# The exits of the second block's three sub-layers in two ranges of 256 tokens

## The chip, the cores and the metric

The kernel runs on one core of a Trainium2 chip. The metric is the device time of one execution in microseconds (us). TensorE (PE, with its weight loads as PEld), VectorE (DVE), ScalarE (ACT) and GpSimd (POOL) each work through their own instructions in order and wait for each other through semaphores. SyncE (SP) issues the weight transfers.

## The reference

A float32 model on 512 tokens of width 1024 (`D`), two blocks of two layers each. What matters here is the second block. Each of its layers has three sub-layers: a gated feed-forward network of width 2816, a token mixer (a state-space part and attention), and a second feed-forward network.

```
def pre(x_in, i):
    return rms_norm(x_in, norm_pre[l, i]) * (1.0 + mod[:, i, 1]) + mod[:, i, 0]
def post_add(x_in, y, i, res_w):
    return x_in + res_w * mod[:, i, 2] * rms_norm(y, norm_post[l, i])
x = post_add(x, swiglu(pre(x, 0), ffn_w_in[l, 0], ffn_w_out[l, 0]), 0, FFN_RES)
y = token_mixer(pre(x, 1), ...)
x = post_add(x, y, 1, 1.0)
x = post_add(x, swiglu(pre(x, 2), ffn_w_in[l, 1], ffn_w_out[l, 1]), 2, FFN_RES)
```

Both norms take, for each token, a mean of squares over all 1024 channels. So the last of the eight output tiles of a sub-layer must be there before the root of any token is known.

## The kernel before

The activations lie with channels on the partitions: `xT` is 8 tiles (index k or m) of 128 channels x 512 tokens. A matrix product in near-float32 is three matmuls for each pair of 128x128 weights and 128x512 activations (`mm3`, lines 166 to 168: low weights with high activations, high with low, high with high). The split activations of a sub-layer's input are `xh` and `xl`. The weights come in blocks of up to 1024 columns through a ring of four slots: SP fetches (L136), ScalarE makes the high part (`hi`, L150), GpSimd subtracts it for the low part (`w_lo`, L160), TensorE uses the slot and raises `ring.used`.

An exit is what lies between the last output product of a sub-layer and the first products of the next. There are six: three in each layer, and the last of them has no next sub-layer. Its steps are these.

- TensorE makes output tile m = 0 to 7 into a PSUM bank. A feed-forward tile is 22 triples of matmuls (4 weight blocks of 6, 6, 5 and 5 triples), a mixer tile 8 triples (one block).
- For each tile ScalarE (`take_y`, L2140 to L2143) writes `y` (scaled), `ysq` and `sqt` (squares); VectorE multiplies `ycr` = y * xT (`cross`, L2419) and adds the products of the tiles before the last into `tot_ycr`, `tot_ysq`, `tot_sq` (`added`, L2378 and L2430). `y_added` counts this.
- TensorE sums totals and last tile over the partitions with a matrix of ones (`last_sums`, `sums`, L1852), 512 tokens in four groups of 128 which land in 32 partitions each.
- ScalarE takes the root (L2147), VectorE the reciprocal (L2464), TensorE spreads it over all partitions (`spread_root`, L1861). From the same sums VectorE works out the mean square of the new x in five small operations (L2468 to L2474), then root (L2155), reciprocal (L2476) and spread once more for the next sub-layer's input norm.
- For each tile k VectorE runs four operations of 512 columns: `part` (y times spread root, from PSUM, L2481), `added` (into xT, L2493), `scaled` (L2500, into `th_s`) and `low` (L2458, into `xl`); between the last two ScalarE writes `xh` (`shift`, L2164). The order is part, added, scaled of tile k+1 and then low of tile k. `low` raises `h_split`.
- TensorE starts the next sub-layer's first four weight columns (`products`): for k = 0 to 5 all four banks, then bank by bank k = 6 and 7. It waits for `h_split` at each new k, and frees the ring's slots with k = 7.

ScalarE's order at a feed-forward exit is: `hi` of the next sub-layer's weight blocks 0 to 2, `take_y` of tile 7, root, root, `hi` of block 3, shifts. In the first feed-forward network of a layer VectorE also prepares constants of the state-space part between the tiles (`prepare`).

Of the kernel before, what the change touches and what calls it, by code (L numbers as in the profile page):

```python
# [13 lines left out]
P = 128  # L14
# [210 lines left out]
def first_block(nc, block, mem, consts, own, prev, after, bank, xT, xh, xl, l, w_in, g_q, w_q_up, g_kv, w_kv_up,  # L225
# [1183 lines left out]
    "h_high", "y_added", "out_turned", "out_written")  # L1409
# [8 lines left out]
class SecondSignals(Signals):  # L1418
# [3 lines left out]
    def __init__(self, nc, ctx, ring, tag, layer, mixer):  # L1422
        Signals.__init__(self, nc, ctx, ring, tag)
        self.s = {x: self.sem(x) for x in SECOND_SIGNALS}
        self.s.update(mixer)
        self.since = {x: n * layer for x, n in MIXER_SIGNALS.items()}
        self.bank_used = None


def second_block(nc, block, mem, consts, own, prev, after, carried, out, bank, xT, xh, xl, l, mod_b, norm_pre,  # L1430
# [6 lines left out]
    E0 = 0 if prev is None else 1  # L1437

# [107 lines left out]
    for label, b in (("sq0", 7), ("ysq0", 6), ("ycr0", 5), ("post0", 4), ("pre1", 7)):  # L1546
        hold(label, b)
# [45 lines left out]
    for label, b in (("sq1", 7), ("ysq1", 6), ("ycr1", 5), ("post1", 4), ("pre2", 7)):  # L1593
        hold(label, b)
    hold_loop("in1", range(4), FT // 2)
    hold_loop("out1", range(2), KT // 2)
    if after is None:
        hold("sq2", 7)
        hold("post2", 4)
        for k, b in enumerate((0, 1, 2, 3, 5, 6, 7, 0)):  # L1600
            hold(("out", k), b)
    else:
        hold("vec_next", 5)
        for label, b in (("sq2", 7), ("ysq2", 6), ("ycr2", 5), ("post2", 4), ("pre3", 7)):
            hold(label, b)
# [212 lines left out]
    def _(pe):  # L1818
# [16 lines left out]
        def products(labels, n0, x, x_lo, at, banks=None):  # L1835

            banks = banks or [free(pe, label) for label in labels]
            order = [(k, b) for k in range(KT - 2) for b in range(4)] + [(k, b) for b in range(4) for k in (KT - 2, KT - 1)]
            for k, b in order:
                if b == 0:  # L1840
                    pe.wait_ge(s["h_split"], at + k + 1)
                wh, wl = weights(n0 + b, b) if k == 0 else (ring.hi[b], ring.lo[b])
                cc = slice(k * P, k * P + P)
                last = mm3(nc, banks[b], wh[:, cc], wl[:, cc], x[:, k, :], x_lo[:, k, :], k == 0, k == KT - 1)
                if k == KT - 1:
                    last.then_inc(ring.used, 1)
# [8 lines left out]
        def spread_root(n, label, r):  # L1855

            out = free(pe, label)
            pe.wait_ge(s["root_ready"], n)
            for g in range(TT):
                one_row = ident[:, 32 * g:32 * g + 1].broadcast_to([P, P])  # L1860
                last = nc.tensor.matmul(out[:, g * P:(g + 1) * P], one_row, r, start=True, stop=True)  # L1861
            last.then_inc(s["root_spread"], 1)

        def entry_norm():
# [5 lines left out]
            spread_root(1, "pre0", pre_r)  # L1870

        def last_sums(i):

            pe.wait_ge(s["y_added"], 6 * i + 6)
            for label, x in ([("ysq", ysq), ("ycr", ycr), ("sq", sqt)] if i < EXITS else [("sq", sqt)]):
                sums(free(pe, f"{label}{i}"), tot[label], True, False)
            for label, x in ([("ysq", ysq), ("ycr", ycr), ("sq", sqt)] if i < EXITS else [("sq", sqt)]):
                if label == "sq":
                    pe.wait_ge(*taken(i, KT - 1))
                else:  # L1880
                    pe.wait_ge(s["y_square" if label == "ysq" else "y_cross"], 8 * i + KT)
# [18 lines left out]
        def ffn(sub):  # L1900
# [13 lines left out]
            products(None, B_IN[sub], xh, xl, 16 * sub, bank[0:4])  # L1914
            with nc.tensor.Fori(1, FT // 2) as i:
                hidden(i)
            for m in range(KT):
# [12 lines left out]
            exit_norm(2 * sub)  # L1930
# [3 lines left out]
        products([("u", t) for t in range(4)], B_U, xh, xl, 8)  # L1934
# [166 lines left out]
        for m in range(KT):  # L2101
            product(free(pe, ("mo", m)), B_MO + m, m % 4, KT, MH, ML, wait=s["merged"] if m == 0 else None, at=since["merged"]).then_inc(ring.used, 1)
        exit_norm(1)
        ffn(1)
        if after is None:
            for k in range(KT):
                pe.wait_ge(s["y_sum"], 8 * 2 + k + 1)
# [6 lines left out]
    def _(act):  # L2114
# [18 lines left out]
        def take_y(i, m, src):  # L2133
# [3 lines left out]
            elif m == 0 and i:  # L2137
                act.wait_ge(s["mean_ready"], i + 1 - E0)
# [10 lines left out]
        def exit_norm(i):  # L2149

            act.wait_ge(s["mean_ready"], i + 2 - E0)
            root(post_r, f"sq{i}")
            if i < EXITS:
                act.wait_ge(s["new_mean"], i + 1)
                nc.scalar.activation(pre_r, ms[:, :], ACT.Sqrt, bias=eps[:, 0:1]).then_inc(s["pre_std"], 1)  # L2155

        def shift(i, k):

            to, at = stage(i)
            if k < KT - 1:  # L2160
# [20 lines left out]
        def ffn(sub):  # L2181
# [20 lines left out]
            for m in range(KT):  # L2202
                n = b_of + 4 * m
                for b in range(4 if m < KT - 1 else 3):
# [14 lines left out]
            exit_norm(2 * sub)  # L2219
            hi(b_of + 4 * KT + 3)  # L2220

        if prev is None:
# [8 lines left out]
            shifts(0)  # L2231
        ffn(0)
        shifts(1)
# [120 lines left out]
        for m in range(KT):  # L2354
            act.wait_ge(ring.used, B_MO + m + 1)
            read(take_y(1, m, held(("mo", m))), ("mo", m))
            if m < KT - 1:
                hi(B_MO + 4 + m)
            if m == 0:
                sqrt_table()  # L2360
        exit_norm(1)
# [580 lines left out]
```

## Time and profile before

| what | value |
| --- | --- |
| median of 3 runs | 3354.19 us (3351.44 to 3356.36) |
| profiled execution, its own time | 3349.84 us |
| profiled execution, span | 3348.0 us |
| mean granted TensorE clock | 0.975 of full speed |
| TensorE / VectorE busy | 96% / 62% of the span |

The profile is of one execution. Times within it are microseconds from the start of the span. A matmul's record is longer than its share of the engine, because matmuls overlap; the distance from start to start is what counts.

### The profile page before, as it was taken

The numbers are of one execution on the slowest core, as the hardware profiler recorded it, in microseconds if no ns is written. First come the engines' busy times: TensorE is split into PE (matmuls) and PEld (weight loads), VectorE is DVE, ScalarE is ACT, GpSimd is POOL, SyncE is SP. The second block draws the span as 40 slices with busy tenths as digits, with TensorE's granted clock in tenths as the row PEclk, the third lists the DMA queues.
The fourth block names the chain that finished last, engine by engine and source line by source line (L and its number), as shares of the span: only waits on it lengthen the run. The fifth ranks groups of instructions, "written<-read, shape, count | busy, mean of one in ns | idle before, by whom it ended". The sixth has DMA issues, their size and how long they took to land.

```text
span 3348.0 us, 43790 instructions
## 1 busy us (share of the span) xinstructions
PE 3199.6 (96%) x16130; PEld 2534.0 (76%) x16130; DVE 2070.9 (62%) x2722; ACT 1162.9 (35%) x1798; POOL 1337.2 (40%) x569
## 2 busy tenths in 40 slices
PE   8999999999996999899998999999998999989998
PEld 6757787757775888787677888878887876878887
DVE  3777785777785445898377443464459964774422
ACT  3355323355323223333434222422233335332233
POOL 3402343402333445544153445634464531534454
PEclk9999999999997999999999999999998999999999
DMA  4524472624553332667142332333235871423332
GB/s 128 186 82 126 145 226 74 190 74 130 151 176 93 98 94 82 97 112 102 55 122 64 114 94 84 103 88 100 85 92 82 129 103 33 142 76 100 92 86 73
DMA packets 577892, 358.73 MB, mean 107 GB/s; under 512 B 50946, under 2 KB 528588, under 8 KB 577484
## 3 DMA queue, kind: packets, MB, share of 16 engines
q1 hardware_dynamic: 573908, 350.23, 40.7%
q10 hardware_dynamic: 3832, 6.42, 0.5%
q8 instruction: 102, 1.67, 0.2%
q14 instruction: 50, 0.41, 0.0%
HBM read 343.75 MB, written 10.49 MB: 106 GB/s over the span
## 4 chain that ended last, share of the span: by engine, by line
PE 57%; DVE 7%; DMA 2%; SPq 1%; POOL 1%; ACT 1%; issue 1%; ACTq 0%; POOLq 0%; DVEq 0%
PE bank L166 18%; PE bank L168 17%; PE bank L167 17%; DMA w_raw<-in_mix_w_in_dram 2%; SPq L1754 1%; POOL w_lo L160 1%; DVE xT L2493 1%; DVE w_s L2378 1%; PE bank L2059 1%; PE bank L2038 1%; PE bank L2071 0%; PE bank L2018 0%; DVE y_s L2481 0%; DVE th_s L2500 0%; PE bank L2034 0%
## 5 line engine op out<-in xcount | busy, mean ns | idle before, releaser
L160 POOL TENSOR_TENSOR w_lo<-w_raw,w_hi 128x1024 fp32r<-128x1024 f32 (+1 forms) x556 | 1329.2, 2396 | 1975.2 <-ACT w_hi L150 1972.4
L166 PE MATMUL bank<-xh,w_lo 128*128 128x512 f32 x2432 | 973.8, 400 | 47.2 <-DVE xl L2458 28.1
L167 PE MATMUL bank<-xl,w_hi 128*128 128x512 f32 x2432 | 955.7, 393 | 0.0
L168 PE MATMUL bank<-xh,w_hi 128*128 128x512 f32 x2432 | 955.6, 393 | 0.0
L150 ACT ACTIVATE w_hi<-w_raw 128x1024 fp32r<-128x1024 f32 (+1 forms) x556 | 566.1, 1021 | 781.6 <-PE bank L168 673.4
L166 PEld LDWEIGHTS bank<-xh,w_lo 128*128 128x128 f32 x2432 | 462.4, 190 | 162.2 <-issue 47.5
L167 PEld LDWEIGHTS bank<-xl,w_hi 128*128 128x128 f32 x2432 | 463.0, 190 | 98.4 <-issue 4.8
L168 PEld LDWEIGHTS bank<-xh,w_hi 128*128 128x128 f32 x2432 | 461.8, 190 | 98.5
L166 PE MATMUL bank<-HH_s,w_lo 128*128 128x512 f32 x704 | 274.2, 389 | 0.0
L168 PE MATMUL bank<-HH_s,w_hi 128*128 128x512 f32 x704 | 273.9, 389 | 0.0
L167 PE MATMUL bank<-HL_s,w_hi 128*128 128x512 f32 x704 | 273.9, 389 | 0.0
L2613 DVE TENSOR_TENSOR th_s<-th_s,bank 128x512 f32<-128x512 f32 x88 | 60.5, 688 | 317.1 <-PE bank L168 316.0
L2617 DVE SCALAR_TENSOR_TENSOR HL_s<-th_s,HH_s 128x512 f32 x88 | 242.6, 2756 | 10.9
L2189 ACT ACTIVATE th_s<-bank 128x512 f32<-128x512 f32 x88 | 52.7, 599 | 383.2 <-PE bank L168 353.7
L2610 DVE SCALAR_TENSOR_TENSOR th_s<-th_s,bank 128x512 f32<-128x512 f32 x88 | 60.5, 687 | 171.9 <-ACT th_s L2189 171.9
L1146 DVE SCALAR_TENSOR_TENSOR macc_b_l<-m_raw_l,cs_l,macc_b_l 128x512 f32<-128x512 f32 x168 | 160.8, 957 | 4.7
L167 PEld LDWEIGHTS bank<-HL_s,w_hi 128*128 128x128 f32 x704 | 132.2, 188 | 27.5
L166 PEld LDWEIGHTS bank<-HH_s,w_lo 128*128 128x128 f32 x704 | 132.2, 188 | 27.5
L168 PEld LDWEIGHTS bank<-HH_s,w_hi 128*128 128x128 f32 x704 | 132.2, 188 | 27.2
L2430 DVE TENSOR_TENSOR tot_sq_s<-tot_sq_s,sqt_s 128x512 f32<-128x512 f32 x36 | 89.9, 2496 | 94.1 <-ACT sqt_s L2143 93.1
L2419 DVE TENSOR_TENSOR ycr_s<-y_s,xT 128x512 f32<-128x512 f32 x35 | 48.6, 1389 | 112.8 <-ACT y_s L2140 112.6
L1146 DVE SCALAR_TENSOR_TENSOR macc_a_l<-m_raw_l,cs_l,macc_a_l 128x512 f32<-128x512 f32 x56 | 66.1, 1180 | 13.0 <-DMA m_raw_l<-in_mod_w_dram 11.2
(509 smaller groups left out, 4276.1 us busy)
## 6 DMA issues: line engine op xcount, KB each, us to landing
w_raw<-in_ffn_w_in_dram SPq DMA_DIRECT2D x176, 512.0 KB, 3.8
m_raw_l<-in_mod_w_dram SPq DMA_DIRECT2D x128, 512.0 KB, 5.0
w_raw<-in_w_in_dram SPq DMA_DIRECT2D x78, 512.0 KB, 4.0
w_raw<-in_mix_w_in_dram SPq DMA_DIRECT2D x64, 512.0 KB, 9.7
w_raw<-in_ffn_w_out_dram SPq DMA_DIRECT2D x64, 384.0 KB, 3.4
w_raw<-in_ffn_w_out_dram SPq DMA_DIRECT2D x64, 320.0 KB, 3.2
m_half_l<-in_mod_w_dram SPq DMA_DIRECT2D x32, 256.0 KB, 2.8
w_raw<-in_w_out_dram SPq DMA_DIRECT2D x16, 512.0 KB, 4.7
```

Source lines behind the costliest of these rows:

```text
L150: ins = nc.scalar.activation(to(ring.hi[s]), of(ring.raw[s]), ACT.Copy)
L160: ins = nc.gpsimd.tensor_tensor(to(ring.lo[s]), of(ring.raw[s]), to(ring.hi[s]).bitcast(F32), ALU.subtract)
L166: nc.tensor.matmul(out, wl, xh, start=start, stop=False)
L167: nc.tensor.matmul(out, wh, xl, start=False, stop=False)
L168: return nc.tensor.matmul(out, wh, xh, start=False, stop=stop)
L1146: ins = V.scalar_tensor_tensor(macc[:, :], w, cc, macc[:, :], ALU.mult, ALU.add)
L2189: nc.scalar.activation(th[v][:, :], bank[2 * v], ACT.Tanh, scale=0.5).then_inc(s["tanh"], 1)
L2419: V.tensor_tensor(to[:, :], y[:, m, :], xT[:, m, :], MUL).then_inc(s["y_cross"], 1)
L2430: V.tensor_tensor(tot["sq"][:, :], tot["sq"][:, :], sqt[m % 2][:, :], ADD).then_inc(s["y_added"], 1)
L2610: V.scalar_tensor_tensor(t[:, :], t[:, :], 1.0, bank[2 * v], ADD, MUL).then_inc(evac[2 * v], 1)
L2613: V.tensor_tensor(t[:, :], t[:, :], bank[2 * v + 1], MUL).then_inc(evac[2 * v + 1], 1)
L2617: V.scalar_tensor_tensor(HL[:, to, :], t[:, None, :], 0.5, HH[:, to, :].bitcast(F32), MUL, SUB).then_inc(s["hidden"], 1)
```

## The change

Everything at an exit that took 512 tokens now takes a range of 256 (`tok[0]`, `tok[1]`), once for each half `hf`.

- The last output tile (`TAIL` = 7) is made in two passes over the same weights, the first into its old bank and the second into another bank (`tail`). Sums, roots and spreads of half 0 are put between the matmuls of half 1.
- ScalarE takes the halves of the last tile with two sets of three operations. At a feed-forward exit `hi` of the next blocks 0 to 2 now comes after the first root: block 0 between the two roots of half 0, blocks 1 and 2 after them, block 3 between the shifts.
- The three sums share one bank. A spread is made for each half.
- VectorE runs part, added, scaled and low on 256 columns, all 8 tiles of half 0 and then all 8 of half 1. The last tile's second `cross_half`, the root work of half 1 (after tile 2) and its second reciprocal (after tile 4) stand between them.
- `products` goes through the 32 pairs of tile and weight column twice, with matmuls of 256 columns: for half 0 in an order in which columns 2 and 3 lag by one and two tiles, with the sums and spreads of half 1 of the exit behind steps 7, 15 and 23. The entry of the first layer goes in halves too.

```diff
 def products(labels, n0, x, x_lo, at, banks=None, tail=None):
...
+            for hf in range(2):
+                if hf == 0:
+                    order = sorted(((k, b) for k in range(KT) for b in range(4)), key=lambda kb: (kb[0] + (0, 0, 1, 2)[kb[1]], kb[1]))
+                else:
+                    order = [(k, b) for k in range(KT - 2) for b in range(4)] + [(k, b) for b in range(4) for k in (KT - 2, KT - 1)]
+                split = 0
+                for i, (k, b) in enumerate(order):
+                    if k + 1 > split:
+                        split = k + 1
+                        pe.wait_ge(s["h_split"], at + 8 * hf + split)
+                    wh, wl = weights(n0 + b, b) if k == hf == 0 else (ring.hi[b], ring.lo[b])
+                    cc = slice(k * P, k * P + P)
+                    last = mm3(nc, banks[b][:, tok[hf]], wh[:, cc], wl[:, cc], x[:, k, tok[hf]], x_lo[:, k, tok[hf]], k == 0, k == KT - 1)
+                    if hf and k == KT - 1:
+                        last.then_inc(ring.used, 1)
+                    if tail is not None and hf == 0 and i in (7, 15, 23):
+                        tail((i - 7) // 8)
...
 # TensorE, feed-forward exit
+            for hf in range(2):
+                out = free(pe, f"tail{i}") if hf else bank[TAIL % 2]
+                for b in range(4):
+                    wh, wl = weights(4 * TAIL + B_OF[sub] + b, b)
+                    for k in range(CUT[b], CUT[b + 1]):
+                        cc = slice((k - CUT[b]) * P, (k - CUT[b] + 1) * P)
+                        last = mm3(nc, out[:, tok[hf]], wh[:, cc], wl[:, cc], HH[:, k, tok[hf]], HL[:, k, tok[hf]], k == 0, k == FT - 1)
+                        if hf and (b, k - CUT[b]) == (3, 2):
+                            first_half(i, 2)
+                    if hf:
+                        last.then_inc(ring.used, 1)
+                        if b < 2:
+                            first_half(i, b)
...
 # TensorE, mixer exit
+        for hf in range(2):
+            out = free(pe, "tail1" if hf else ("mo", TAIL))
+            for k in range(KT):
...
+                if hf and k == 4:
+                    first_half(1, 0)
...
+        first_half(1, 1)
+        first_half(1, 2)
...
 # ScalarE
+        def exit_tail(i, src, splits, last, done):
+            take_half(i, 0, src)
+            post_root(i, 0)
+            for n in splits[0:1]:
+                hi(n)
+            if i < EXITS:
+                pre_root(i, 0)
+            for n in splits[1:3]:
+                hi(n)
+            act.wait_ge(ring.used, done)
+            take_half(i, 1, src)
...
+            shift(i + 1, 0, 0)
+            hi(last)
+            shift(i + 1, 0, 1)
+            shift(i + 1, 0, 2)
+            post_root(i, 1)
+            shift(i + 1, 0, 3)
+            shift(i + 1, 0, 4)
+            pre_root(i, 1)
...
 # VectorE
+            pre_root(i, 0)
+            dve.wait_ge(s["root_spread"], 1 - E0 + root_count(i, 1))
+            part(0, 0)
+            added(0, 0)
+            dve.wait_ge(s["root_spread"], 1 - E0 + root_count(i, 2))
+            scaled(0, 0)
+            cross_half(i, 1)
+            order = [(hf, k) for hf in range(2) for k in range(KT)]
+            for n, item in enumerate(order):
+                if n + 1 < len(order):
+                    if n + 1 == KT:
+                        dve.wait_ge(s["root_spread"], 1 - E0 + root_count(i, 4))
+                    part(*order[n + 1])
+                    added(*order[n + 1])
+                    scaled(*order[n + 1])
+                low(i + 1, *item)
+                if item == (0, 2):
+                    post_root(i, 1)
+                if item == (0, 4):
+                    pre_root(i, 1)
```

`first_half(i, step)` is, on TensorE, the sums (step 0), the first spread (1) and the second spread (2) of half 0; the `tail` argument does the same for half 1.

## Rows read from the trace of the kernel before

**Rows 1.** The page: engines and the chain that ended last.
```profile
PE 3199.6 (96%) x16130; PEld 2534.0 (76%) x16130; DVE 2070.9 (62%) x2722; ACT 1162.9 (35%) x1798; POOL 1337.2 (40%) x569
PE 57%; DVE 7%; DMA 2%; SPq 1%; POOL 1%; ACT 1%; issue 1%; ACTq 0%; POOLq 0%; DVEq 0%
```
**Rows 2.** TensorE's waits, whole span: total us, times, longest.
```profile
PE bank L166 <- DVE xl L2458: 28.1, 6, 5.5
...
PE bank L2059 <- ACT PT_s L2330: 10.7, 4, 5.3
```
**Rows 3.** Timeline of layer 0's first exit: start, duration, [idle before].
```profile
1403.84 2.82 DVE L2430 TENSOR_TENSOR tot_sq_s<-tot_sq_s,sqt_s 128x512 f32<-128x512 f32 x1
...
1404.80 0.39 PE L168 MATMUL bank<-HH_s,w_hi 128*128 128x512 f32 x1
...
1406.63 2.36 POOL L160 TENSOR_TENSOR w_lo<-w_raw,w_hi 128x1024 fp32r<-128x1024 f32 x1 [0.52 <-ACT w_hi L150]
...
1407.15 2.39 DVE L2419 TENSOR_TENSOR ycr_s<-y_s,xT 128x512 f32<-128x512 f32 x1 [0.49 <-ACT y_s L2140]
...
1410.70 0.95 DVE L2464 RECIPROCAL rstd_s<-rstd_s 128x128 f32<-128x128 f32 x1 [1.17 <-ACT rstd_s L2147]
...
1413.69 0.95 DVE L2476 RECIPROCAL rstd_s<-rstd_s 128x128 f32<-128x128 f32 x1 [0.47 <-ACT rstd_s L2155]
...
1421.53 0.76 PE L166 MATMUL bank<-xh,w_lo 128*128 128x512 f32 x1 [4.70 <-DVE xl L2458]
```
**Rows 4.** VectorE's timeline, one round of the loop over tiles.
```profile
1425.40 0.75 DVE L2500 SCALAR_TENSOR_TENSOR th_s<-xT,pre_s,bank 128x512 f32<-128x512 f32 x1
1426.07 0.75 DVE L2458 SCALAR_TENSOR_TENSOR xl<-th_s,modc,xh 128x512 fp32r<-128x512 f32 x1
1426.73 0.68 DVE L2481 TENSOR_TENSOR y_s<-y_s,bank 128x512 f32<-128x512 f32 x1
1427.44 0.69 DVE L2493 TENSOR_TENSOR xT<-xT,y_s 128x512 f32<-128x512 f32 x1
1428.17 0.75 DVE L2500 SCALAR_TENSOR_TENSOR th_s<-xT,pre_s,bank 128x512 f32<-128x512 f32 x1
```
**Rows 5.** VectorE's groups by shape: operations of 256 columns; busy, mean ns.
```profile
L2378 DVE TENSOR_TENSOR b_s<-fr_s,Bi_s 128x256 f32<-128x256 f32 x2 | 5.0, 2506 | 0.1
...
L2378 DVE TENSOR_TENSOR b_s<-fi_s,Bi_s 128x256 f32<-128x256 f32 x2 | 0.9, 426 | 0.1
```
**Rows 6.** Timeline at full clock: eight weight loads of a spread, their eight matmuls.
```profile
1806.68 0.97 PEld L1861 LDWEIGHTS bank<-rstd_s,tables_sb 128*128 128x128 f32 x8 [1.81 <-issue]
1806.71 1.13 PE L1861 MATMUL bank<-rstd_s,tables_sb 128*128 128x128 f32 x8 [1.57 <-DVE rstd_s L2464]
```
**Rows 7.** Last totals at a mixer exit and at layer 0's last exit (timeline).
```profile
1800.45 2.83 DVE L2430 TENSOR_TENSOR tot_sq_s<-tot_sq_s,sqt_s 128x512 f32<-128x512 f32 x1
...
2169.12 2.77 DVE L2430 TENSOR_TENSOR tot_sq_s<-tot_sq_s,sqt_s 128x512 f32<-128x512 f32 x1
```
**Rows 8.** Output matmuls of those exits by source line; first and last start.
```profile
L168 PE MATMUL bank<-MH_s,w_hi x19: 388/389/389, 1790.2 to 1802.5; 128*128 128x512 f32 x19
...
L168 PE MATMUL bank<-HH_s,w_hi x27: 388/389/389, 2160.3 to 2177.9; 128*128 128x512 f32 x27
```
**Rows 9.** The chain of work: first products, their end, the next weights.
```profile
1445.09 0.87 PE bank L1939 x8
...
1816.44 0.77 PE bank L166
...
1838.13 2.41 POOL w_lo L160
...
2191.89 0.77 PE bank L166
```
**Rows 10.** VectorE's timeline in the mixer, its longest wait before attention.
```profile
1545.39 0.69 DVE L2730 COPY Xr_s<-rho_s 128x1024 f32<-128x1024 f32 x1 [2.72 <-PE bank L2002]
```
**Rows 11.** Stretch of the first products: us, engines' busy time, granted clock (PEclk).
```profile
1421.50:1425.00 3.50, 3.47 (x9) 2.78 (x10) 3.40 (x6) 0.73 (x1) 0.00 (x0) 0.54 0.87 197
```

More of the change, by code:

```diff
@@ L1833, in product, with products @@
             return last
-        def products(labels, n0, x, x_lo, at, banks=None):
+        def products(labels, n0, x, x_lo, at, banks=None, tail=None):
             banks = banks or [free(pe, label) for label in labels]
[L1838 to L1846, printed above, removed]
+            for hf in range(2):
[15 more added lines that the diff above has]
+                        tail((i - 7) // 8)
         def sums(out, x, start, stop):
@@ L1853, in sums, with spread_half @@
             return last
[L1855 to L1861, printed above, removed]
+        def spread_half(hf, label, r):
+            out = free(pe, f"{label}{hf}")
+            h = rows_of[hf]
+            for g in (2 * hf, 2 * hf + 1):
+                one_row = ident[h, 32 * g:32 * g + 1].broadcast_to([P // 2, P])
+                last = nc.tensor.matmul(out[:, g * P:(g + 1) * P], one_row, r[h, :], start=True, stop=True)
             last.then_inc(s["root_spread"], 1)
@@ L1913, in ffn @@
                     pe.wait_ge(prev.evac[b], prev.bank_used[b])
-            products(None, B_IN[sub], xh, xl, 16 * sub, bank[0:4])
+            products(None, B_IN[sub], xh, xl, 32 * sub, bank[0:4],
+                     second_half(1) if sub else prev.tail if prev is not None else None)
             with nc.tensor.Fori(1, FT // 2) as i:
                 hidden(i)
-            for m in range(KT):
+            for m in range(TAIL):
                 pe.wait_ge(evac[m % 2], m // 2 + turn[f"out{sub}"][m % 2])
@@ L2218, in ffn @@
                     sqrt_table()
-            exit_norm(2 * sub)
-            hi(b_of + 4 * KT + 3)
+            n = b_of + 4 * TAIL
+            exit_tail(2 * sub, bank[TAIL % 2], [n + 4 + b for b in range(3)], n + 7, n + 4)
         if prev is None:
@@ L2230, in _ @@
                 hi(B_IN[0] + n)
-            shifts(0)
+            for hf in range(2):
+                for k in range(KT):
+                    shift(0, hf, k)
         ffn(0)
-        shifts(1)
         for t in range(4):
@@ L2633, in ffn @@
                 if part < EXITS:
-                    cross(part, m)
+                    if m == TAIL:
+                        cross_half(part, 0)
+                    else:
+                        cross(part, m)
                 if part == 2 and m == 0 and after is not None:
```

340 lines of the change are left out of this document (221 added, 119 removed).

## Prediction

> **What bounds the kernel now.** I read the page first: TensorE is busy 96% of the span, and the chain that ended last is mostly its matmuls; VectorE is busy 62% [rows 1]. So only what adds or removes TensorE time, or holds TensorE up, counts. Then TensorE's waits: the longest is for `low` (`xl`), 28.1 us in 6 waits, the entry and the five exits that have a next sub-layer [rows 2]. The timeline of one exit shows a serial chain: last matmul, ScalarE, sums, root, reciprocal, root, reciprocal, part, added, scaled, shift, low, first product [rows 3].
>
> I count from T, the start of the last output tile. Matmuls of 512 columns follow each other every 0.227 us (26 triples from 2160.3 to 2177.9, 18 from 1790.2 to 1802.5 [rows 8]); a feed-forward tile takes 66 x 0.227 = 15.0 us, a mixer tile 5.45. T is 1390.05 at a layer's first exit (A), 1797.3 at the mixer exit (B), 2163.15 at layer 0's last (C) [rows 3, 8]. The first product starts at T+31.5, T+19.1 and T+28.7 [rows 3, 9]. There are two A, two B, one C, and the last exit D without a next input.
>
> The next four columns then take 23.6 us, 1421.53 to 1445.09 [rows 3, 9], of which 96 matmuls, 21.8 us at 0.227, are TensorE's own work. VectorE feeds them at the distances 0.67, 0.66, 0.71 and 0.73 us, 2.77 us for each tile [rows 4], against 12 x 0.227 = 2.72 us of TensorE. They are level. That balance is what the change touches.
>
> **TensorE's price of halves.** No row has a split-precision matmul of 256 columns. Below it is half of 0.227, 0.114 us. Above it is 0.227, if weight loads of 128 columns could not go faster. Against that: eight loads with their eight matmuls follow at (0.97 - 0.19)/7 = 0.111 us [rows 6]. Keeping the fixed part of 0.227, I take 0.120: a feed-forward tail grows from 15.0 to 15.8 us, a mixer tail from 5.45 to 5.8, the four columns from 21.8 to 23.0.
>
> The Trainium skill (TensorE: Matmul & The Clock Gate, Back-to-back issue gap) gives N/2.4 + 2.5 ns, 109 ns for 256 columns. By it my sum below would be some 5 us less.
>
> **VectorE's price of halves.** An operation of 256 columns takes 0.426 us where 512 take 0.69 [rows 4, 5]: 0.265 less, not half. Each of the four distances shrinks by 0.267, so a half tile costs 2.77 - 1.07 = 1.70 us against 12 x 0.120 = 1.44 us on TensorE. VectorE becomes the pacer. Sixteen half tiles, from the first `low` to the last: 14 x 1.70 + 0.4 = 24.2 us. In between, new in this place:
> - after `low` of tile 2, VectorE waits for half 1's sums, which TensorE reaches only behind three more triples: 1.1 + 0.2 + sums 0.7 + root and hand-overs 0.6 = 2.6 us;
> - reciprocal 0.95 and the five mean operations, 3.0 us from reciprocal to reciprocal less 0.45 for the root [rows 3]: 2.5 us;
> - the second reciprocal: 1.0 us;
> - before half 1, the last spread, behind step 23: 1.1 + 0.2 + 0.45 + 0.15 = 1.9 us;
> - after the last `low`, seven triples on TensorE: 0.2 + 21 x 0.120 = 2.7 us.
> The sum is 24.2 + 2.6 + 2.5 + 1.0 + 1.9 + 2.7 = 34.9 us against 23.6: **+11.3 us** at each of five exits. ScalarE's shifts lie beside this (0.5 of each 1.70 us). TensorE waits meanwhile and hides its own surcharge.
>
> **When the columns start.** At A the totals of tile 6 end at 1406.66 = T+16.6 [rows 3], because `prepare` holds VectorE. The new half sums stand behind the first block of half 1 (T+10.1), so TensorE waits there and the tail ends near T+25, no longer T+15. Sums, root and reciprocal end at T+19.1, the second reciprocal 3.0 us later, and part, added, scaled, the second cross (which needs `take_half` behind two `hi` of 1.06 us) and the first round bring the first product to T+27.5. At C the totals are ready (2171.9 = T+8.7 [rows 7]); the same steps give T+20.4. At B they are ready at 1803.3 = T+6.0 [rows 7], behind which the same chain gives T+15.4: a short tail hides little.
>
> These times suppose that GpSimd is not in the way. It is: an operation of VectorE with two SBUF operands that starts while GpSimd splits weights takes 2.39 us and ends 0.55 after it [rows 3], and the same form of 256 columns takes 2.506 instead of 0.426 [rows 5]: 2.1 us lost for each meeting. Before, three of the four splits lay beside the long tail. Now `hi` of blocks 0 to 2 comes after the first root, so all four (2.4 us each) fall on the mean operations, `added`, cross and `low`. Bounds: none met (+0) and three to four effective (+6.0 at A and C), one at B (+2.2). I take two thirds at A and C and the one at B: starts T+31.5, T+24.5, T+17.6, against T+31.5, T+28.7, T+19.1. So the start gains 0, 4.2 and 1.5 us.
>
> The Trainium skill (SBUF — State Buffer, Terms) has VectorE and GpSimd share a port pair that is held for the full instruction, the loser blocked. If every overlap costs as it says, A and C start 2 us later and the sum is some 6 us more.
>
> **Other terms.**
> - At A the mixer's VectorE work begins later: the last `low` ends at T+63.7 (31.5 + 34.9 - 2.7), before at T+48.8 (31.5 - 0.2 and 6 x 2.77 + 0.9 for the seven other tiles). Of these 14.9 us a wait of 2.72 [rows 10] takes up; then attention waits for VectorE's chain already (10.7 us of TensorE's waits are behind it [rows 2]). So A costs 12.2, not 11.3.
> - The ring: before, column 0 was done 6 triples (4.1 us) ahead of the end, and `hi` 1.06 plus `w_lo`, ending at 1840.54 [rows 9], just fill that. Now it is 6 half triples, 2.2 us: TensorE waits 1.9 us more at B (two), C and the entry; at A the transposes of 0.87 [rows 9] cover half, 1.0.
> - The entry: 1.2 more on TensorE, 0.7 earlier start: +0.5.
> - D: tail +0.8, half 0's sums and spread on TensorE +0.9, shorter chain for half 1 -1.1, VectorE's extra operation for each of eight tiles (2 x 0.426 - 0.69 = 0.16) +1.2: +1.8.
> - More semaphores and one bank for three sums: nothing, they lie beside.
>
> **Sum.** A 2 x 12.2 = 24.4; B 2 x (11.3 - 1.5) = 19.6; C 11.3 - 4.2 = 7.1; ring 4 x 1.9 + 2 x 1.0 = 9.6; entry 0.5; D 1.8: +63.0. B's and C's columns took some 0.4 more than A's before (a longer slow stretch), 1.2 in all: **+62 us**. The profiled execution took 3349.84, 4.35 below the median; on the median 3354.2 + 62 = **3416 us**.
>
> **Rivals.**
> 1. *GpSimd is rarely met*: the bound of none. 2 x 4.0 + 4.1 + 2 x 2.2 = 16.5 less: 3400. For it: which operation gets in first is a matter of tenths of a microsecond. Against: three of the four `hi` have their data early.
> 2. *All splits meet, and the clock falls.* TensorE at the first products had 0.54, the 1.2 GHz level, for 3.5 us after it had been mostly waiting [rows 11]. Cold halves cost 0.213 instead of 0.120, and the 24 ahead of half 1's sums lengthen VectorE's wait by 1.6 us in five places. With 6 us of splits: +14, 3430.
> 3. *VectorE does not pace*: faster. If a half tile took VectorE under 1.44 us and half 1's roots were met ready, the columns would take TensorE's 23.0 us; then only the starts count, 4.2 + 2 x 1.5 earlier plus 16.5 without meetings, less ring, entry and D, 11.9: 12 us faster, 3342. The point is 1.44 us a half tile. Against: four times 0.36 is below any such operation in the rows.
> 4. *Weight loads bind* at 0.19 to 0.227 for 256 columns: tails longer by up to 14 us and columns by TensorE's 40 us instead of 34.9: near 3510. Against: 0.111 in rows 6.
> 5. *It cancels*: earlier starts at all exits and little waiting inside the columns leave the time within 0.2%.
>
> **How the numbers follow.** Forecast 0.50, rival 1 0.20, rival 2 0.15, rival 3 0.07, rival 4 0.04, cancelled 0.04. About 0.2% (7 us) is what a measurement of this kernel can tell from no change. Faster 0.07, same 0.04, slower 0.89. The range holds the first three: below, rival 1 with halves at 0.114 and no ring wait, 3400 - 5 - 10 and some 5 for the waits inside the columns, 3380; above, rival 2 and as much again of slow clock, 3440.
>
> **What would show it.** Between the first half product and the last, VectorE's four operations near 1.70 us a round and TensorE idle a good part; a VectorE wait of some 2.6 us after the third `low`; operations of 256 columns with 2 us and more beside GpSimd's splits; half matmuls 0.12 us apart; at A the half sums waiting for `tot_sq`. I am wrong if the rounds take under 1.5 us, if TensorE's waits for `xl` fall below 28.1 us in total, or if the columns take under 30 us.

## The result, and the profile after

The changed kernel took 3424.66 us (median of 4 runs, 3420.72 to 3427.28) against 3353.29 (3351.44 to 3356.36): ratio 1.0211, 95% interval 1.0193 to 1.0229. It is 71.4 us slower; 62 were forecast, 3416 us, in a range of 3380 to 3440. Its profiled execution took 3423.56 us with a span of 3421.8, 73.8 more than the span before.

The page, engines and the chain that ended last, answers to [rows 1]:
```profile
PE 3246.0 (95%) x17018; PEld 2612.3 (76%) x17018; DVE 2118.8 (62%) x2947; ACT 1183.9 (35%) x1874; POOL 1342.7 (39%) x569
...
PE 54%; DVE 14%; issue 1%; ACT 1%; POOL 0%; DMA 0%; ACTq 0%; POOLq 0%; DVEq 0%
```
VectorE's busy share is still 62%, but its share of the chain went from 7% to 14%: a share of busy time did not show this, the chain does. TensorE's waits over the span (total us, times, longest), against [rows 2]:
```profile
PE bank L166 <- DVE xl L2602: 62.7, 20, 7.2
...
PE bank L166 <- POOL w_lo L160: 17.1, 11, 4.3
...
PE bank L1903 <- DVE tot_sq_s L2569: 7.2, 4, 2.3
PE bank L2065 <- ACT Btr_s L2424: 6.9, 2, 3.9
...
PE bank L2136 <- ACT PT_s L2468: 1.2, 4, 0.4
```
The kernel before had, beside the waits of [rows 2]:
```profile
PE bank L166 <- POOL w_lo L160: 7.1, 6, 4.3
...
PE bank L1852 <- DVE tot_sq_s L2430: 3.9, 4, 1.5
```
The wait for `low` has more than doubled and comes 20 times instead of 6. The wait for GpSimd's `w_lo` went from 7.1 to 17.1 us. The half sums inside the tail wait for `tot_sq`, as forecast, 7.2 us in 4 waits. The 10.7 us ahead of attention have shrunk to 1.2, but 6.9 us of waiting for `Btr_s`, a table of the state-space part, are new in the mixer.

VectorE's timeline at layer 0's first exit (A1; the two layers' exits are A1, B1, C, then A2, B2 and the last, D), against [rows 3, 4] (T, the start of the last output tile, is 1396.64 here):
```profile
1408.34 0.69 DVE L2569 TENSOR_TENSOR tot_sq_s<-tot_sq_s,sqt_s 128x512 f32<-128x512 f32 x1
1409.06 0.42 DVE L2558 TENSOR_TENSOR ycr_s<-y_s,xT 128x256 f32<-128x256 f32 x1
1411.79 0.94 DVE L2611 RECIPROCAL rstd_s<-rstd_s 64x128 f32<-64x128 f32 x1 [2.30 <-ACT rstd_s L2257]
...
1413.40 1.98 DVE L2511 TENSOR_TENSOR ms_t_s<-ms_t_s,rstd_s 64x128 f32<-64x128 f32 x1
...
1417.68 2.48 DVE L2681 TENSOR_TENSOR xT<-xT,y_s 128x256 f32<-128x256 f32 x1
...
1420.67 1.98 DVE L2558 TENSOR_TENSOR ycr_s<-y_s,xT 128x256 f32<-128x256 f32 x1
...
1423.01 2.12 DVE L2681 TENSOR_TENSOR xT<-xT,y_s 128x256 f32<-128x256 f32 x1
...
1425.56 0.48 DVE L2602 SCALAR_TENSOR_TENSOR xl<-th_s,modc,xh 128x256 fp32r<-128x256 f32 x1
...
1427.26 0.48 DVE L2602 SCALAR_TENSOR_TENSOR xl<-th_s,modc,xh 128x256 fp32r<-128x256 f32 x1
...
1428.96 0.48 DVE L2602 SCALAR_TENSOR_TENSOR xl<-th_s,modc,xh 128x256 fp32r<-128x256 f32 x1
1433.19 0.95 DVE L2611 RECIPROCAL rstd_s<-rstd_s 64x128 f32<-64x128 f32 x1 [3.75 <-ACT rstd_s L2257]
```
Read three things. The rounds of a half tile are 1.70 us apart (1425.56, 1427.26, 1428.96). Four operations, each with two SBUF operands, take 1.98 to 2.48 us, although 0.29 to 0.42 is their own time where no split runs beside them: the meetings with GpSimd's splits. And behind the third `low`, VectorE stands 3.75 us for half 1's sums. The rest of these columns (timeline of TensorE, with VectorE's wait for the last spread and ScalarE's first reading of column 0):
```profile
1426.29 0.55 PE L166 MATMUL bank<-xh,w_lo 128*128 128x256 f32 x1 [6.49 <-DVE xl L2602]
1426.64 0.41 PE L167 MATMUL bank<-xl,w_hi 128*128 128x256 f32 x1
...
1430.44 0.28 PE L166 MATMUL bank<-xh,w_lo 128*128 128x256 f32 x1
...
1437.58 0.58 PE L166 MATMUL bank<-xh,w_lo 128*128 128x256 f32 x1 [4.29 <-DVE xl L2602]
...
1446.02 0.42 DVE L2668 TENSOR_TENSOR y_s<-y_s,bank 128x256 f32<-128x256 f32 x1 [2.28 <-PE bank L1881]
...
1461.11 0.60 ACT L2375 ACTIVATE us_s<-bank 128x512 f32<-128x512 f32 x1 [1.23 <-PE bank L168]
...
1463.07 1.03 PE L2016 MATMUL bank<-tables_sb,crow_s 128*128 128x128 f32 x8
```
The first 17 half matmuls follow at 0.21 us, then the distance falls to 0.12. The stretches show why (us, busy times of the engines, granted clock, DMA share, GB/s), against [rows 11]:
```profile
1426.30:1430.30 4.00, 4.00 (x17) 3.82 (x18) 3.00 (x8) 0.51 (x1) 0.00 (x0) 0.50 0.98 59
1430.30:1431.20 0.90, 0.90 (x8) 0.80 (x7) 0.00 (x0) 0.00 (x0) 0.00 (x0) 0.99 0.48 75
```
A granted clock of 0.50 is the 1.2 GHz level, after 6.49 us of waiting; half 1's sums stand behind just these matmuls. At the other four exits the slow level lasts longer: 9.0, 5.6, 6.1 and 8.1 us from the first product (B1, C, A2, B2), so that nearly all of the 24 matmuls ahead of those sums run at it, and it comes back after the later waits inside the columns.

At A1 the four columns take 1426.29 to 1463.07, 36.8 us; 23.6 before, 34.9 forecast. That is the exit nearest to the forecast: B1, C, A2 and B2 took 41.2, 38.1, 38.3 and 40.6 us, where they had taken 23.9 each. For the table one mark serves all exits: from T to ScalarE's first reading of column 0's products, in two parts, to the first product and from there. It comes from the timelines of both kernels. The kernels of the experiments are in the same table.

| kernel | A1 | B1 | C | A2 | B2 |
|---|---|---|---|---|---|
| before | 31.5 + 19.5 | 19.2 + 20.0 | 28.7 + 20.0 | 31.8 + 20.0 | 19.2 + 20.0 |
| after | 29.7 + 34.8 | 16.0 + 39.2 | 26.6 + 36.1 | 29.0 + 36.3 | 15.6 + 38.6 |
| vector_in_halves | 32.5 + 23.6 | 19.3 + 23.6 | 28.8 + 23.6 | 32.0 + 23.6 | 19.3 + 23.6 |
| sums_ahead | 28.8 + 28.9 | 15.4 + 30.7 | 26.4 + 29.0 | 29.4 + 29.0 | 15.9 + 34.7 |
| one_operation_less | 27.9 + 25.6 | 15.9 + 26.7 | 25.5 + 25.6 | 27.8 + 25.6 | 15.3 + 29.8 |
| after_no_low | 24.5 + 37.5 | 14.5 + 35.8 | 22.2 + 36.3 | 24.5 + 34.7 | 14.2 + 34.9 |
| before_no_low | 30.4 + 20.4 | 17.4 + 19.5 | 27.8 + 20.2 | 28.5 + 20.0 | 18.3 + 20.2 |
| columns_whole | 37.4 + 19.7 | 25.4 + 20.7 | 32.5 + 20.1 | 36.2 + 19.6 | 27.1 + 20.2 |
| whole_spreads_late | 35.2 + 20.8 | 24.7 + 20.4 | 32.7 + 19.9 | 36.4 + 19.4 | 24.5 + 19.5 |
| one_root | 31.7 + 19.9 | 19.9 + 20.0 | 31.0 + 20.5 | 31.7 + 20.3 | 19.9 + 20.1 |

The first product comes 2 to 4 us sooner after the change, and everything behind it 15 to 19 us later. Sums against before: A +13.5 twice, B +16.1 and +15.0, C +14.1, 72.2 in all. Between A's first reading and B's T there are 353.75 and 352.17 us instead of 356.24 and 356.78, 7.1 back. The last exit is +2.2, the entry's first column +2.3 from its first product. The first product of the entry is 4.3 later, and that is not the change's: ScalarE's root there starts at 1037.99 instead of 1033.38, ahead of the first instruction that was changed, and lies between 1030.8 and 1038.9 in the profiles of this study. 72.2 - 7.1 + 2.2 + 2.3 + 4.3 = 73.9: but for rounding the difference of the spans, 73.8.

### The profile page after: what moved, and what is told of

It reads as the page before. It is cut to its first block, busy times and chain, and to the rows that moved or that the text cites. A ratio compares the mean times of both kernels' runs of the same rounds, so it can differ in the third digit from the quotient of the medians.

```text
span 3421.8 us, 45914 instructions
## 1 busy us (share of the span) xinstructions
PE 3246.0 (95%) x17018; PEld 2612.3 (76%) x17018; DVE 2118.8 (62%) x2947; ACT 1183.9 (35%) x1874; POOL 1342.7 (39%) x569
## 4 chain that ended last, share of the span: by engine, by line
PE 54%; DVE 14%; issue 1%; ACT 1%; POOL 0%; DMA 0%; ACTq 0%; POOLq 0%; DVEq 0%
PE bank L166 17%; PE bank L168 16%; PE bank L167 16%; DVE w_s L2511 2%; DVE xT L2681 1%; DVE ct_s L2511 1%; DVE tt_s L2511 1%; DVE z_s L2511 1%; DVE tot_sq_s L2569 1%; PE bank L2115 1%; PE bank L2136 1%; DVE xl L2602 1%; PE bank L1903 1%; PE bank L2095 1%; DVE th_s L2688 1%
## 5 line engine op out<-in xcount | busy, mean ns | idle before, releaser
L166 PE MATMUL bank<-xh,w_lo 128*128 128x512 f32 (+1 forms) x2624 | 1019.6, 389 | 91.4 <-DVE xl L2602 62.7
L167 PE MATMUL bank<-xl,w_hi 128*128 128x512 f32 (+1 forms) x2624 | 997.3, 380 | 0.0
L168 PE MATMUL bank<-xh,w_hi 128*128 128x512 f32 (+1 forms) x2624 | 996.7, 380 | 0.0
L166 PEld LDWEIGHTS bank<-xh,w_lo 128*128 128x128 f32 x2624 | 509.3, 194 | 203.4 <-issue 53.0
L167 PEld LDWEIGHTS bank<-xl,w_hi 128*128 128x128 f32 x2624 | 510.4, 195 | 90.3 <-issue 5.1
L168 PEld LDWEIGHTS bank<-xh,w_hi 128*128 128x128 f32 x2624 | 509.4, 194 | 89.9
L166 PE MATMUL bank<-HH_s,w_lo 128*128 128x512 f32 (+1 forms) x792 | 291.3, 368 | 0.0
L167 PE MATMUL bank<-HL_s,w_hi 128*128 128x512 f32 (+1 forms) x792 | 289.8, 366 | 0.0
L168 PE MATMUL bank<-HH_s,w_hi 128*128 128x512 f32 (+1 forms) x792 | 289.7, 366 | 0.0
L2810 DVE SCALAR_TENSOR_TENSOR HL_s<-th_s,HH_s 128x512 f32 x88 | 242.5, 2756 | 10.9
L168 PEld LDWEIGHTS bank<-HH_s,w_hi 128*128 128x128 f32 x792 | 149.8, 189 | 23.9
L2277 ACT ACTIVATE xh<-th_s,modc 128x256 fp32r<-128x256 f32 x96 | 48.8, 509 | 134.6 <-DVE th_s L2688 124.4
```

Of the source, the lines that this page charges most:

```text
L166: nc.tensor.matmul(out, wl, xh, start=start, stop=False)
L167: nc.tensor.matmul(out, wh, xl, start=False, stop=False)
L168: return nc.tensor.matmul(out, wh, xh, start=False, stop=stop)
L2810: V.scalar_tensor_tensor(HL[:, to, :], t[:, None, :], 0.5, HH[:, to, :].bitcast(F32), MUL, SUB).then_inc(s["hidden"], 1)
```

## The experiments

**1. VectorE and ScalarE in halves, in the kernel before.**
```diff
+    pieces = [(k, hf) for k in range(KT) for hf in range(2)]
...
-                    pe.wait_ge(s["h_split"], at + k + 1)
+                    pe.wait_ge(s["h_split"], 2 * (at + k + 1))
...
+            for n, item in enumerate(pieces):
+                if n + 1 < len(pieces):
+                    part(*pieces[n + 1])
+                    added(*pieces[n + 1])
+                    scaled(*pieces[n + 1])
+                low(i + 1, *item)
```


> The kernel before, with only VectorE's and ScalarE's work behind each root (part, added, scaled, shift, low) in operations of 256 columns, tile by tile; roots, sums and TensorE's matmuls stay whole. My theory (VectorE paces the first four columns, 1.70 us for a half tile): 16 rounds where 8 of 2.77 us were, so some 5 us more at each of five exits, a little less at the two ahead of attention: about 3378 us (3370 to 3388), with TensorE's waits for low near 50 us. The rival that VectorE does not pace: within 5 us of before, 3353 to 3358.

Measured: 3378.41 us, 1.0074 (1.0057 to 1.0090), 26 us more. VectorE's rounds (timeline) and TensorE's waits:
```profile
1427.26 0.48 DVE L2464 SCALAR_TENSOR_TENSOR xl<-th_s,modc,xh 128x256 fp32r<-128x256 f32 x1
1427.65 0.41 DVE L2488 TENSOR_TENSOR y_s<-y_s,bank 128x256 f32<-128x256 f32 x1
1428.10 0.42 DVE L2501 TENSOR_TENSOR xT<-xT,y_s 128x256 f32<-128x256 f32 x1
1428.56 0.48 DVE L2509 SCALAR_TENSOR_TENSOR th_s<-xT,pre_s,bank 128x256 f32<-128x256 f32 x1
1428.96 0.48 DVE L2464 SCALAR_TENSOR_TENSOR xl<-th_s,modc,xh 128x256 fp32r<-128x256 f32 x1
```
```profile
PE bank L166 <- DVE xl L2464: 43.5, 24, 5.7
```
Roots, sums and matmuls are as before, and 3.6 to 4.1 us are lost between first product and first reading at each exit. A further 3.2 us are lost at each A between that reading and B's T, where a wait of TensorE's for `Btr_s`, 2.9 us, is new. TensorE's waits for `low` are 43.5 us, for some 50 expected. So the size of the operations behind the roots (VectorE's four, and ScalarE's shift with them) alone costs some 25 of the 71 us.

**2. The changed kernel with whole columns.**
```diff
-            for hf in range(2):
...
+                for n in range(3):
+                    tail(n)
...
+            for k, b in order:
...
+            post_root(i, 0)
...
+                pre_root(i, 0)
+                cross_half(i, 1)
+            post_root(i, 1)
...
+                pre_root(i, 1)
```


> The changed kernel with its last output tile, sums and roots in two ranges kept, but the normalised tiles and the first four columns whole again, behind both ranges' roots. My theory: the columns fall from some 37 us back to 23.6, while the start moves back behind half 1's roots (about 13 us behind the end of the tail): start at T+36, T+20.5 and T+32 at A, B and C against T+31.5, T+19.1 and T+28.7 before, +15 in all, and the last exit +2: about 3370 us (3360 to 3380). The rival that the split tail itself carries the loss: 3400 or more.

Measured: 3377.85 us (3366.34 to 3383.43), 1.0067 (1.0043 to 1.0092): 47 us less than the changed kernel. The columns are back at some 20 us to the first reading; the starts stand at T+37.4, T+25.4 and T+32.5, later than I expected at B by 5. TensorE waits for roots inside the tail, which puts the tail's end off; experiment 8 asks whether that is what holds the start.

**3. Half 1's sums ahead of the products, in the changed kernel.**
```diff
+            if tail is not None:
+                tail(0)
             for hf in range(2):
...
-                    if tail is not None and hf == 0 and i in (7, 15, 23):
-                        tail((i - 7) // 8)
+                    if tail is not None and hf == 0 and i in (12, 16):
+                        tail((i - 8) // 4)
```


> The changed kernel with half 1's sums ahead of the first half product instead of behind eight triples, and its two spreads behind the triples 13 and 17 instead of 16 and 24. If the waits inside the columns (3.75 to 5.2 us for the sums of half 1, 2.3 to 3.1 us for the last spread) come from TensorE's order, they shrink to under 1 us each: 25 to 30 us less, about 3397 us (3390 to 3403). The rival that they come from the work on VectorE and ScalarE itself, and only change their name: 3415 to 3425.

Measured: 3391.18 us (3390.59 to 3394.20), 1.0114 (1.0097 to 1.0131), 33.5 us less than the changed kernel. VectorE's timeline at the place of the 3.75 us wait, and the wait for `low` over the span:
```profile
1430.83 0.48 DVE L2604 SCALAR_TENSOR_TENSOR xl<-th_s,modc,xh 128x256 fp32r<-128x256 f32 x1
1431.34 0.95 DVE L2613 RECIPROCAL rstd_s<-rstd_s 64x128 f32<-64x128 f32 x1
1432.32 0.29 DVE L2618 TENSOR_TENSOR ms_t_s<-bank,rstd_s 64x128 f32<-64x128 f32 x1
```
```profile
PE bank L166 <- DVE xl L2604: 27.1, 15, 3.8
```
The reciprocal follows its `low` at once. Nothing was made shorter, three items of TensorE's queue were moved: the waits were an effect of order. From first product to end the columns now take 30.9 us at A1, C and A2; the prediction's sum without its two waits is 34.9 - 2.6 - 1.9 = 30.4. The slow clock went back with the waits: 23 to 34 half matmuls of the columns run at the slow distance, where it had been 38 to 59, except at B2 with 57 of them, whose columns take 36.7 us. So some of the 33.5 us is clock.

**4. The price of half matmuls, in the kernel before.**
```diff
-                    product(bank[b], n, b, KT, xh, xl).then_inc(ring.used, 1)
+                    for c in (slice(0, T // 2), slice(T // 2, T)):
+                        for k in range(KT):
+                            last = mm3(nc, bank[b][:, c], wh[:, cc], wl[:, cc], xh[:, k, c], xl[:, k, c], k == 0, k == KT - 1)
```


> The kernel before, with the 40 weight blocks of each feed-forward loop that TensorE alone sets the time of (3840 matmuls of 512 columns in all) done as two runs of 256 columns, each with its own weight loads: a price for the half matmul. At my 0.120 us: 3840 x (0.240 - 0.227) = +50 us, 3403. At exactly half, 0.114: 3357. At 0.109: 3320. If weight loads bind at 0.19 to 0.227: 590 to 870 us more.

Measured: 3402.09 us (3401.02 to 3406.93), 1.0146 (1.0129 to 1.0163), 49.9 us more: 13.0 ns for each of the 3840 pairs. The timeline, start by start:
```profile
1100.13 0.28 PE L166 MATMUL bank<-xh,w_lo 128*128 128x256 f32 x1
1100.25 0.28 PE L167 MATMUL bank<-xl,w_hi 128*128 128x256 f32 x1
1100.37 0.28 PE L168 MATMUL bank<-xh,w_hi 128*128 128x256 f32 x1
```
The distance is 0.120 us at full clock. Weight loads of 128 columns do not bind at 256.

**5. One of VectorE's four operations less**, on top of the kernel of 3 (tiles 1 to 6 of each half leave out the addition of y to x).
```diff
             def added(hf, k):
+                if 0 < k < KT - 1:
+                    return
```


> The kernel with half 1's sums ahead (3391.18 us), where the tiles 1 to 6 of each half leave out VectorE's addition of y to x (the output differs), one of the four operations of a round: 3 x 0.426 = 1.28 us a round against TensorE's 1.44. If VectorE paces the half columns: 12 rounds x (1.70 - 1.44) = 3.1 us less at each of five exits, about 3376 us (3370 to 3380). If TensorE paces them, nothing changes: 3388 to 3394.

Measured: 3359.12 us (3355.44 to 3366.56), 32 us less than with the operation; against before 1.0025 (1.0014 to 1.0035). Both theories missed the size, and the direction is the first's. The rounds (timeline) are 1.12 us, shorter than TensorE's 1.44:
```profile
1423.14 0.48 DVE L2604 SCALAR_TENSOR_TENSOR xl<-th_s,modc,xh 128x256 fp32r<-128x256 f32 x1
1423.53 0.41 DVE L2670 TENSOR_TENSOR y_s<-y_s,bank 128x256 f32<-128x256 f32 x1
1423.86 0.47 DVE L2693 SCALAR_TENSOR_TENSOR th_s<-xT,pre_s,bank 128x256 f32<-128x256 f32 x1
1424.26 0.47 DVE L2604 SCALAR_TENSOR_TENSOR xl<-th_s,modc,xh 128x256 fp32r<-128x256 f32 x1
```
From first product to first reading it saves 3.3, 4.0, 3.4, 3.4 and 4.9 us, near the 3.1 expected. The rest lies in starts that are 0.9 to 1.5 us earlier at the feed-forward exits, and in 4.7 and 6.7 us between A's first reading and B's T: TensorE's waits there fall from 10.6 to 6.4 and from 10.9 to 5.4 us, above all those for `Btr_s` (3.9 and 4.2), which are gone. What VectorE finishes earlier at A helps the mixer behind it.

**6. and 7. GpSimd's splits cut to one column** at the four blocks behind each exit (`four` runs `split_lo` with `ONE_COLUMN`), in the changed kernel and in the one before.
```diff
+ONE_COLUMN = [(lambda x: x[:, 0:1], lambda x: x[:, 0:1])]
...
-        quads(4, B_G + 4)
+        quads(4, B_U)
+        four(B_U)
+        quads(B_U + 4, B_G + 4)
```


> The changed kernel, with GpSimd's low parts of the four weight blocks behind each exit cut to one column (this leaves out those low parts, so the output differs), TensorE's matmuls unchanged: it takes the meetings of VectorE with GpSimd away, and TensorE's waits for w_lo there. If all four splits cost some 2.1 us of the chain at A and C and one or two at B, as the trace reads: 3 x 7 + 2 x 3 us, and some 12 us of ring waits: about 3388 us (3378 to 3398). If the meetings lie beside other waits, only the ring waits go: 3410 or more.

> The same cut in the kernel before (again without those low parts), as the control: there one meeting at an exit lies on the chain (2.1 us at A and C), and TensorE waits 7.1 us for w_lo: about 3341 us (3335 to 3348). The meetings and ring waits that the change adds are then the difference of the two differences, by my reading some 25 us; by the rival under 8.

Measured: after 3401.59 us (3398.84 to 3403.76), 23.1 less; before 3342.42 (3337.68 to 3347.75), 10.3 less, 0.9972 (0.9960 to 0.9983). The first misses its range of 3378 to 3398, and neither expectation read the edit right. It leaves TensorE's waits for `w_lo` behind the columns, 1.2 to 2.1 us at each exit, as they were, since those are for the next four blocks. What it prices is the meetings alone: the change adds 12.8 us of them. In the kernel before I had counted one meeting on the chain at A and at C; its trace has more: the first `xT` at all five exits and the cross at both A, 1.7 us each, 12 us together, where the run gives 10.3 back. In the changed kernel the blocked operations lose 24 us together, and the run gives 23.1 back.

Exit by exit the two don't agree so well. The start moved by 4.4 to 5.1 us at A and C, where four operations had lost 6.9 together (at C: 1.67 + 2.02 + 1.56 + 1.69, each less its own 0.29 or 0.42), and by 1.4 to 1.5 at B. VectorE's operations did lose their 2 us: `xT` at C is 0.43. But VectorE then waits for TensorE's spread and for ScalarE's `y` (timelines of VectorE and TensorE at C):
```profile
2207.21 0.43 DVE L2692 TENSOR_TENSOR xT<-xT,y_s 128x256 f32<-128x256 f32 x1
2209.29 0.48 DVE L2699 SCALAR_TENSOR_TENSOR th_s<-xT,pre_s,bank 128x256 f32<-128x256 f32 x1 [1.66 <-PE bank L1892]
2210.71 0.42 DVE L2569 TENSOR_TENSOR ycr_s<-y_s,xT 128x256 f32<-128x256 f32 x1 [0.93 <-ACT y_s L2255]
...
2213.09 0.55 PE L166 MATMUL bank<-xh,w_lo 128*128 128x256 f32 x1 [2.92 <-POOL w_lo L160]
```
6.94 - 1.66 - 0.93 = 4.35, and the start moved by 4.4. The wait put down to `w_lo` is for block 3's `hi` on ScalarE; it ends only 0.15 us behind the first `low`.

**8. Whole columns, with half 0's spreads and all of half 1's sums and spreads behind the tail.**
```diff
                     if hf:
                         last.then_inc(ring.used, 1)
-                        if b < 2:
-                            first_half(i, b)
+                        if b == 0:
+                            first_half(i, 0)
...
+            second_half(i)(0)
+            for step in (1, 2):
+                first_half(i, step)
+            for step in (1, 2):
+                second_half(i)(step)
```


> As the kernel with split tail and whole columns (3377.85 us), but TensorE doesn't wait for half 0's roots inside the tail: half 0's spreads and all of half 1's sums and spreads stand behind the tail. There TensorE waited 23.8 us in 15 places for the roots, and the tail's end stood behind them. If that order moved the start back: about 3350 us (3343 to 3358), no slower than before. If the chain of two roots on VectorE is what sets the start: 3370 or more.

Measured: 3373.61 us (3363.91 to 3378.05), 1.0054 (1.0036 to 1.0073). My 3350 was wrong. The start moved by 2.2 us or less at four exits and by 2.6 at B2: T+35.2, 24.7, 32.7, 36.4 and 24.5. VectorE's timeline at the first exit says why:
```profile
1409.15 0.94 DVE L2592 RECIPROCAL rstd_s<-rstd_s 64x128 f32<-64x128 f32 x1 [1.62 <-ACT rstd_s L2253]
...
1413.81 0.94 DVE L2612 RECIPROCAL rstd_s<-rstd_s 64x128 f32<-64x128 f32 x1 [0.47 <-ACT rstd_s L2263]
1416.06 1.45 DVE L2545 TENSOR_TENSOR ycr_s<-y_s,xT 128x256 f32<-128x256 f32 x1 [1.31 <-ACT y_s L2240]
1418.86 0.95 DVE L2592 RECIPROCAL rstd_s<-rstd_s 64x128 f32<-64x128 f32 x1 [1.35 <-ACT rstd_s L2253]
...
1421.83 0.95 DVE L2612 RECIPROCAL rstd_s<-rstd_s 64x128 f32<-64x128 f32 x1 [0.46 <-ACT rstd_s L2263]
```
A reciprocal over 64 partitions takes 0.94 us, as long as one over 128 [rows 3]. Splitting by partitions halves nothing: half 1's chain is as long as the whole one was, and half 0's is extra.

**9. The split tail with one root**, to tell the split tail from the split roots: one set of sums behind the tail, one post root and one pre root. `both` is TensorE's sums and spreads over all 128 partitions. The edit also puts ScalarE's `hi` of three blocks back ahead of the second half's reading, so against experiment 8 two things differ.
```diff
-                            first_half(i, b)
...
+            both(i)
...
-            post_root(i, 0)
-            for n in splits[0:1]:
-                hi(n)
-            if i < EXITS:
-                pre_root(i, 0)
-            for n in splits[1:3]:
+            for n in splits:
                 hi(n)
             act.wait_ge(ring.used, done)
             take_half(i, 1, src)
+            post_root(i)
```


> The split tail alone: the last output tile in two ranges of 256 tokens and ScalarE's three reads of each, but one set of sums behind the tail, one post root and one pre root over all 128 partitions, whole tiles and whole columns. If it is the two chains of roots on VectorE, and TensorE's stop in the tail for half 0's sums, that put the start back by 4 to 5 us in the kernels with whole columns (T+35 to 37, T+24.5 to 27 and T+32.6 at A, B and C), the start comes to the tail's T+15.5 (B: 5.6) and 13.1 us of chain: T+28.6 to 29.5, T+18.7, T+28.6, and the time to 3345 to 3355 us, level with before. If the halved tail itself costs (its matmuls, its splits that come late), it stays at 3362 or more.

Measured in 11 runs against 15: 3352.64 us (3347.46 to 3355.64) against 3352.97, ratio 0.9999 (0.9990 to 1.0008): level with before. The starts missed at the feed-forward exits (T+31.7 and T+31.0; I had 28.6 to 29.5), with this in the way (VectorE's timeline at the first exit):
```profile
1405.58 4.99 DVE L2542 TENSOR_TENSOR ycr_s<-y_s,xT 128x256 f32<-128x256 f32 x2
1411.92 0.95 DVE L2589 RECIPROCAL rstd_s<-rstd_s 128x128 f32<-128x128 f32 x1 [1.35 <-ACT rstd_s L2256]
...
1416.44 2.43 DVE L2632 TENSOR_TENSOR xT<-xT,y_s 128x512 f32<-128x512 f32 x1
```
The two cross halves, 0.42 us each, took 4.99 us together: they met splits, which GpSimd ran from 1402.60 to 1410.30. In this form the split tail gains nothing, and it costs nothing that could be measured. That the splits fall there because the blocks of the ring come free only with half 1 is my reading of the order, not tested.

## Why the prediction was right

**VectorE paces the half columns: right.** 1.70 us a round, forecast 1.70; it costs 26 us alone (experiment 1), and taking an operation away shortens the columns by about the amount at which TensorE takes over (5). 256 columns take 0.42 us where 512 take 0.69. The Trainium skill (VectorE: DVE Perf Modes, The TRN2 errata) gives (N + 151)/0.96 ns for such an operation, 691 and 424 ns: the trace agrees, and a half keeps over 60% of the price.

**TensorE's price: right.** 0.120 us (4), so rival 4, that weight loads bind, is out. The 109 ns that the Trainium skill (TensorE: Matmul & The Clock Gate, Back-to-back issue gap) gives for 256 columns, as the gap of a matmul by itself, set against the measured 0.227 us of 512, would by estimate have made experiment 4 about 35 us faster than before; it was 49.9 slower.

**The columns: 34.9 forecast, 36.8 to 41.2 measured.** Two terms were too small. The wait for half 1's sums, 2.6, was 3.75, 5.24, 4.44, 4.62 and 4.82 (A1, B1, C, A2, B2); the wait for the last spread, 1.9, was 2.3 to 3.1. Over the five exits that is 13.6 us more than forecast. The slow clock of rival 2 is there, and longer than the rival had it. At A1 17 half matmuls at 0.213 instead of 0.120 are 1.6 us more ahead of those sums, the rival's own figure; at the other four nearly all 24 are slow, some 2 us. At B a meeting of VectorE with a split, 1.7 us, falls inside the columns too. No run changed the clock alone, so its share is read, not tested. That these waits are TensorE's order is shown (3): with the order changed they went but for one of 2.0 us at B2, and 33.5 us with them.

**The starts.** A was given no gain and had 1.8 and 2.8; B 1.5 and had 3.1 and 3.6; C 4.2 and had 2.1. The kernel without the splits (6) parts each start into chain and meetings. The chain alone was forecast at T+27.5, 15.4 and 20.4 (A, B, C) and came at T+24.5, 14.2 to 14.5 and 22.2; so it was 3.0 us too long at A, and 1.8 too short at C, where the run shows VectorE waiting 1.66 us for the spread and 0.93 for `y`. At A the totals of tile 6 ended at T+12.4, not T+16.6: ScalarE's `hi` had moved behind the first root, so GpSimd no longer sat on `tot_sq`, 0.69 us where it took 2.82 [rows 3]. I had moved those splits and left what they had blocked as it was. Starts, columns and the column's earlier end together, the first reading comes 13.5 us later at A (forecast 11.3 + 1.9 = 13.2), 15.0 to 16.1 at B (11.7) and 14.1 at C (9.0): 72.2 for a forecast of 58.8. That the total was nearer is in part luck: columns 20 us too short were set off by starts that came 6 us earlier than forecast and by 7 us in the mixer that I had with the other sign.

**Meetings with GpSimd: the price right in total, the count not.** By the trace every split is met at A and C, where I took two thirds: four operations with two SBUF operands each lose 1.6 to 2.1 us. Yet the runs (6) price the meetings ahead of the first product at 5.1, 4.4 and 4.5 us at A1, C and A2 and 1.5 and 1.4 at B, 16.9 together; the forecast took 4.0, 4.1 and 2.2, 16.5 together. Behind some meetings stood other waits. The Trainium skill (SBUF — State Buffer, SBUF: two separate sides) has an operation with two SBUF inputs wait until GpSimd's, if that started first, is done; the trace agrees down to 64x128, 1.98 us instead of 0.29. But blocked time is no loss of the kernel's where the chain has another wait right behind it.

**Attention: the sign failed.** I charged A 0.9 us more, because attention would wait for VectorE's chain. In fact the stretch from A's first reading to B's T got 2.5 and 4.6 us shorter. TensorE's waits in it fell by 2.4 and 2.5 us, from 11.8 and 12.5, although the ring's 1.2 and 1.6 are now among them. Those for `PT_s` went from 10.7 to 1.2 us and those for `th_s` (3.8) went, but new ones for `Btr_s` took 3.9 and 3.0: VectorE's late start is met, earlier in the mixer and for less. The other 2.2 us of layer 1 are TensorE's own busy time, 344.3 to 342.1 us, with a granted clock of 1.00 for 0.99; before, a stretch of 10.2 us ran at 0.50 there. Experiment 5 shows the same coupling from the other side. Why the waits sum to less stays open.

**The ring, D and the entry: right in size.** Waits for `w_lo` rose from 7.1 to 17.1 us, 10.0 for a forecast of 9.6 (2.0 at B, C and the entry, 1.2 and 1.6 at A); D took 2.2 for 1.8; the entry's columns 2.3, for 0.5 and the ring's 1.9.

**The rivals.** Rival 1 (GpSimd rarely met) fell: at all three feed-forward exits every split met, and the starts come 4.4 to 5.1 us sooner without them. Rival 3 (VectorE does not pace) fell in experiment 1. Of rival 2 both parts are in the trace, but the meetings cost 16.9 us at the starts by the runs, where the rival's bounds make 22.4, and the slow clock costs more than it said; the result lies between the forecast and it. Rival 5 (it cancels) fell with the result.

Where the 71 us went: 33.5 come back by moving half 1's sums and spreads (3). Of the remaining 38, about 25 are the halves on VectorE (1). The other 12 or so are what is left for the second root chain, the meetings, the ring and the last exit. Taken one by one, the added meetings (12.8, experiments 6 and 7), the ring's waits (10.0) and the last exit (2.2) are already 25, so the parts overlap, and no run divides them further. No version that computes all of it beats the kernel before; the nearest, the split tail with one root, is level with it.

## What to carry to other kernels

Before splitting a stage to start its consumer sooner, compare the two engines' time for one tile: where they are level, halves make the one with the larger fixed share the pacer, and a start won by 2 to 4 us was paid with 15 to 19. Splitting by partitions shortens nothing, since a reciprocal over 64 partitions costs what one over 128 does (0.94 and 0.95 us), and in an in-order queue the late work's sums must stand ahead of the early work's products. When a step is moved, ask also what its old neighbours do without it: here both the totals and the mixer came out faster than forecast. And when a run is to price a cost, check in its trace that the cost is gone: the ring's waits were still there in experiment 6.

## What was not expected of the hardware

Without the four `w_lo` splits behind each exit the kernel before is 10.3 us faster: GpSimd, never on the chain for more than 1% of the span, costs 0.3%, by the trace through VectorE's operations with two SBUF operands. And the granted clock was 0.50 from the start of the half columns for 4.0 us at A1 (17 matmuls) and 5.6 to 9.0 us at the other exits, so that the work with the most waiting behind it ran at the slow level.
